# Matrix products that read and write their 512 columns in runs of 32 from two halves

## What is computed

```python
h = rmsnorm(x, norm_g)
aq, ak, av, ag, cq, ckv, kr, bg, mg = split(h @ w_in)
oa = rmsnorm(diff_attention(aq, ak, av, positions)) * (1 - lam_init)     # 8 heads
ya = (oa * silu(ag)) @ w_oa
q, kv = rmsnorm(cq) @ w_uq, rmsnorm(ckv) @ w_ukv
ob = mla_attention(q, kv, rope(kr))                                      # 8 heads
yb = (ob * silu(bg)) @ w_ob
merged = sigmoid(ga) * ya + sigmoid(gb) * yb                             # ga, gb = split(mg)
out = rmsnorm(x + merged @ w_out, final_g)
```

## Time and profile before

| | |
|---|---|
| median of the runs | 1429.43 us |
| the profiled execution's own time | 1430.07 us |
| its span from first to last instruction | 1428.1 us |
| TensorE matmul busy, share of the span | 99% |
| VectorE, ScalarE, GpSimd busy | 71%, 49%, 2% |
| mean granted TensorE clock | 0.998 |

### The profile page before, as it was taken

The page is one execution under the profiler, slowest core; times in us unless marked ns, Lnnn a source line. Parts: engine busy times, 40 slices in busy tenths (PEclk is TensorE's granted clock), DMA queues, the critical chain, the costliest instruction groups (busy, mean ns, idle before and its releaser), DMA issues.

```text
span 1428.1 us, 17872 instructions
## 1 busy us (share of the span) xinstructions
PE 1412.6 (99%) x6604; PEld 1174.5 (82%) x6604; DVE 1014.9 (71%) x1376; ACT 703.4 (49%) x890; POOL 29.8 (2%) x52
## 2 busy tenths in 40 slices
PE   8999999999999999999999999999999999999997
PEld 7888888888888888888888878888888888888886
DVE  6967888887877768677767655666676354388966
ACT  7546334444343456665666667555564122224434
POOL 0000000000000000000000000000000000000000
PEclk9999999999999999999999999999999999999999
DMA  8439575767665642222232434322342544617674
GB/s 302 143 125 319 175 265 185 251 198 231 219 203 187 208 126 81 76 82 81 81 85 84 110 104 132 86 69 66 84 137 74 154 127 146 207 45 250 191 258 170
DMA packets 182975, 218.42 MB, mean 153 GB/s; under 512 B 19456, under 2 KB 133248, under 8 KB 182272
## 3 DMA queue, kind: packets, MB, share of 16 engines
q1 hardware_dynamic: 174304, 197.64, 44.4%
q10 hardware_dynamic: 8608, 19.93, 3.8%
HBM read 195.51 MB, written 22.02 MB: 152 GB/s over the span
## 4 chain that ended last, share of the span: by engine, by line
PE 91%; DVE 4%; DMA 2%; ACT 1%; SPq 1%; issue 1%; POOL 0%; DVEq 0%; POOLq 0%; ACTq 0%
PE duo L2098 28%; PE duo L2100 28%; PE duo L2099 28%; PE duo L2151 2%; DMA start_y<-start_columns 1%; PE duo L2125 1%; PE duo L2128 1%; SPq L609 1%; ACT m_hi L885 1%; PE duo L2142 1%; PE duo L2147 1%; PE duo L2144 1%; PE duo L2143 1%; PE duo L2146 1%; PE duo L2581 0%
## 5 line engine op out<-in xcount | busy, mean ns | idle before, releaser
L1374 DVE TENSOR_TENSOR w_lo<-w_raw,w_hi 128x1024 fp32r<-128x1024 f32 (+1 forms) x116 | 135.2, 1167 | 101.6 <-ACT w_hi L780 101.1
L2098 PE MATMUL duo<-h_hi,w_hi 128*128 128x512 f32 x512 | 201.8, 394 | 0.0
L2100 PE MATMUL duo<-h_hi,w_lo 128*128 128x512 f32 x512 | 199.6, 390 | 0.0
L2099 PE MATMUL duo<-h_lo,w_hi 128*128 128x512 f32 x512 | 199.6, 390 | 0.0
L885 ACT ACTIVATE m_hi<-m_raw 128x2048 fp32r<-128x2048 f32 (+1 forms) x66 | 115.5, 1752 | 147.8 <-PE duo L2100 79.4
L780 ACT ACTIVATE w_hi<-w_raw 128x1024 fp32r<-128x1024 f32 (+1 forms) x118 | 119.2, 1011 | 126.5 <-DMA w_raw<-in_w_ob_dram 65.7
L1491 DVE TENSOR_TENSOR m_lo<-m_raw,m_hi 128x2048 fp32r<-128x2048 f32 (+3 forms) x71 | 141.9, 2001 | 29.0 <-ACT m_hi L885 28.8
L2098 PE MATMUL duo<-m_hi,h_hi 128*128 128x512 f32 x368 | 144.6, 393 | 1.6 <-DVE h_lo L1527 0.8
L2100 PE MATMUL duo<-m_hi,h_lo 128*128 128x512 f32 x368 | 143.3, 389 | 0.0
L2098 PE MATMUL duo<-m_hi,s_hi 128*128 128x512 f32 x320 | 124.5, 389 | 0.0
L2100 PE MATMUL duo<-m_hi,s_lo 128*128 128x512 f32 x320 | 124.5, 389 | 0.0
(11 more groups left out here) (320 smaller groups left out, 2953.9 us busy)
## 6 DMA issues: line engine op xcount, KB each, us to landing
m_raw<-in_w_in_dram SPq DMA_DIRECT2D x110, 512.0 KB, 4.5
w_raw<-in_w_in_dram SPq DMA_DIRECT2D x132, 256.0 KB, 3.0
o_raw<-in_w_out_dram SPq DMA_DIRECT2D x32, 512.0 KB, 5.1
spare<-in_w_in_dram SPq DMA_DIRECT2D x17, 512.0 KB, 4.9
h_raw<-in_w_in_dram SPq DMA_DIRECT2D x17, 512.0 KB, 4.8
w_raw<-in_w_oa_dram SPq DMA_DIRECT2D x32, 256.0 KB, 3.4
sig<-gates SPq DMA_DIRECT2D x8, 1024.0 KB, 6.4
w_raw<-in_w_ob_dram SPq DMA_DIRECT2D x32, 256.0 KB, 3.3
```

The costliest lines, as they stand in the source:

```text
L1374: dve.tensor_tensor(w_lo[:, piece.slot, 0:cols], w_raw[:, piece.slot, 0:cols], w_hi[:, piece.slot, 0:cols].bitcast(F32), ALU.subtract).the ...
L2098: pe.matmul(dst, lhs_hi, rhs_hi, start=start, stop=False, skip_group_check=onto)
L2099: pe.matmul(dst, lhs_hi, rhs_lo, start=False, stop=False, skip_group_check=onto)
L2100: return pe.matmul(dst, lhs_lo, rhs_hi, start=False, stop=stop, skip_group_check=onto)
```

## The change

All products of `three`, both score functions, the rotary keys and the feature sums go through a new helper, `multiply`, which rearranges the moving operand and the output in the same way. The 512 columns are taken as two halves of 256; the instruction goes through columns 0 to 31 of the first half, 0 to 31 of the second, 32 to 63 of the first, and so on: 16 runs of 32 (8 runs for the 256-column products). Reading and writing use the same order, so each output column gets the sum that it got before, at the same address. Where the moving operand already has two halves in separate places, these are the two halves. Stationary operands, semaphores, waits, the number and order of instructions, transposes and the other engines' code stay. The second product of the groups is accumulated in the banks as before.

```diff
--- before.py
+++ after.py
@@ -37,6 +37,9 @@
 LAM_INIT = 0.8 - 0.6 * math.exp(-0.3 * 0)
 SLOPE0, SLOPE_RATIO = 2.0 ** (-8.0 / HEADS), 2.0 ** (-8.0 / HEADS)
 NORM_EPS, SUBLN_EPS = 1e-6, 1e-5
+
+
+RUN = 32
 
 
 SLOTS = 4
@@ -2093,11 +2096,21 @@
 
         @block.tensor
         def _(pe):
+            def by_turns(columns):
+                if len(columns.shape) == 3:
+                    return columns.rearrange("p j (c r) -> p c j r", r=RUN)
+                return columns.rearrange("p (j c r) -> p c j r", j=2, r=RUN)
+
+            def multiply(dst, lhs, rhs, start, stop, onto=False):
+                return pe.matmul(
+                    by_turns(dst), lhs, by_turns(rhs), start=start, stop=stop, skip_group_check=onto
+                )
+
             def three(dst, lhs_hi, lhs_lo, rhs_hi, rhs_lo, start, stop, onto=False):
 
-                pe.matmul(dst, lhs_hi, rhs_hi, start=start, stop=False, skip_group_check=onto)
-                pe.matmul(dst, lhs_hi, rhs_lo, start=False, stop=False, skip_group_check=onto)
-                return pe.matmul(dst, lhs_lo, rhs_hi, start=False, stop=stop, skip_group_check=onto)
+                multiply(dst, lhs_hi, rhs_hi, start=start, stop=False, onto=onto)
+                multiply(dst, lhs_hi, rhs_lo, start=False, stop=False, onto=onto)
+                return multiply(dst, lhs_lo, rhs_hi, start=False, stop=stop, onto=onto)
 
             def tile(piece, c0, width=P):
                 return w_hi[:, piece.slot, c0:c0 + width], w_lo[:, piece.slot, c0:c0 + width]
@@ -2122,10 +2135,10 @@
                 q = slice(t * P, (t + 1) * P)
                 for m, dst in enumerate((a, b)):
 
-                    pe.matmul(dst[:, :], qa[:, m, q], ka[:, m, :], start=True, stop=False)
+                    multiply(dst[:, :], qa[:, m, q], ka[:, m, :], start=True, stop=False)
                 for m, dst in enumerate((a, b)):
 
-                    last = pe.matmul(dst[:, :], qa[:, m, q], ka_lo[:, m, :], start=False, stop=True)
+                    last = multiply(dst[:, :], qa[:, m, q], ka_lo[:, m, :], start=False, stop=True)
                 last.then_inc(scored, 1)
 
             def scores_b(h, t, prev):
@@ -2139,12 +2152,12 @@
                     pe.wait_ge(v_kept, TOK + VB_COPIES)
                 q = slice(t * P, (t + 1) * P)
                 dst = SC[t][:, :]
-                pe.matmul(dst, q_hl[:, 0, q], k_hl[:, 0, :], start=True, stop=False)
-                pe.matmul(dst, q_hl[:, 0, q], k_hl[:, 1, :], start=False, stop=False)
-                pe.matmul(dst, q_hl[:, 1, q], k_hl[:, 0, :], start=False, stop=False)
-
-                pe.matmul(dst, qr_hl[:, q], kr_hi[:, :], start=False, stop=False)
-                pe.matmul(dst, qr_hl[:, q], kr_lo[:, :], start=False, stop=True).then_inc(scored, 1)
+                multiply(dst, q_hl[:, 0, q], k_hl[:, 0, :], start=True, stop=False)
+                multiply(dst, q_hl[:, 0, q], k_hl[:, 1, :], start=False, stop=False)
+                multiply(dst, q_hl[:, 1, q], k_hl[:, 0, :], start=False, stop=False)
+
+                multiply(dst, qr_hl[:, q], kr_hi[:, :], start=False, stop=False)
+                multiply(dst, qr_hl[:, q], kr_lo[:, :], start=False, stop=True).then_inc(scored, 1)
 
             def turn(src, dst, done):
                 for k in range(TOK):
@@ -2174,8 +2187,8 @@
                 last.then_inc(pv_done, 1)
 
             def feature_sums(done):
-                pe.matmul(TR[:, :], ones_sq[:, :], vT_hi[:, :], start=True, stop=False)
-                pe.matmul(TR[:, :], ones_sq[:, :], vT_lo[:, :], start=False, stop=True).then_inc(done, 1)
+                multiply(TR[:, :], ones_sq[:, :], vT_hi[:, :], start=True, stop=False)
+                multiply(TR[:, :], ones_sq[:, :], vT_lo[:, :], start=False, stop=True).then_inc(done, 1)
 
             pe.wait_ge(cst_in, 16)
             pe.wait_ge(ones_set, 5)
@@ -2453,10 +2466,10 @@
                     both = w_hi[:, piece.slot, k * P:(k + 1) * P]
                     high = w_hi[:, piece.slot, k * P:k * P + B_ROPE]
                     if kt == 0:
-                        pe.matmul(ACC[1][:, :], both, h_hi[:, kt, :], start=True, stop=False)
-                    last = pe.matmul(ACC[1][LOW, :], high, h_lo[:, kt, :], start=False, stop=False)
+                        multiply(ACC[1][:, :], both, h_hi[:, kt, :], start=True, stop=False)
+                    last = multiply(ACC[1][LOW, :], high, h_lo[:, kt, :], start=False, stop=False)
                     if kt:
-                        last = pe.matmul(ACC[1][:, :], both, h_hi[:, kt, :], start=False, stop=kt == KT - 1)
+                        last = multiply(ACC[1][:, :], both, h_hi[:, kt, :], start=False, stop=kt == KT - 1)
                 last.then_inc(used, 1)
 
             def tail(q):
```

## The result

The changed kernel takes 1479.59 us, the kernel before 1429.47 us in the same comparison: a ratio of 1.0348 with a 95% interval of 1.033 to 1.0366, 50 us slower. The forecast was no change.

The account below looks back on a forecast made before the run. TensorE's queue of products was taken as the bound; 1430.07 us profiled plus 0 for 6144 products, with the runs' median 0.64 us lower, gave 1429.5 us. The whole range was 1352 to 1468 us, holding 0.87.

Parts of the forecast that it names:

- What bounds the kernel: Whole kernel: a queue of TensorE products, priced by the step between starts, 226.7 ns for 512 columns, 120.0 for 256.
- The reading side: Moving operand of each product: fifteen jumps at 512 columns, seven at 256, taken as 0; bounds 0 and 6.25 ns a product.
- The writing side: Output bank of each product: the same jumps, taken as 0; bounds 0, 6.25 ns a product, or below nothing.
- The slower rival: Every product: each jump costs a period or more; 1467 us at one period (chance 0.15), 1504 at two (more than one: 0.13).
- The 0.13 that the range left out above: Chance given to a price of more than one period a jump, on either side; 1504 us at two periods.
- The faster rival: Between products: alternating halves hides the 13.3 ns; all gone 1354 us (chance 0.12), half about 1392 us (part gone 0.06).
- the 13.3 ns: Time every product was taken to cost beside streaming its columns at 0.4167 ns each, whatever its length.
- The disturbed stretches: Steps after each four transposes, ten in 2.32 us instead of 2.27: another order might clear this, about 1425 us; chance 0.04.
- What stays: Weight loads, instruction number, semaphores, product order, result places, other engines' reads, DMAs and the 8 us tail expected unchanged.

Follow-up runs that it names:

- the first bench: Kernel before with 22 groups of 30 unneeded products behind its last, differing in columns, reading or writing order and tile width; 512 columns: 226.7 ns side by side, 236.7 in runs of 32.
- fix16: Kernel before plus groups of 30 unneeded products, moving operand read in runs of 16 from four parts 512 columns apart, all beginning at a multiple of 64; step 242.0 ns.

## Why the prediction was wrong, point by point

**What bounds the kernel** was right: TensorE's steps, all but without cover. 10.0 ns on 5760 products would be 57.6 us; 50 appeared, for the two reasons given with the result, and only the 4.4 us of shorter waits is cover.

**The reading side** is the step that failed. I took 0 for fifteen jumps because the products with two runs of 256 showed none for one. The row was right and was the wrong neighbour. Its jump goes from one multiple of 64 to another, so it keeps the round, as do the runs of 64; it could not show what a jump that breaks it costs. The bounds I put, 0 and one period a jump (6.25 ns), were too narrow: measured are 10.0 ns at 512 columns, and nothing at 256.

**The writing side** was right with 0, by the run that writes in turns alone, but by luck: the row I argued from was one of reading, and on the reading side the same argument failed.

**The slower rival** had the direction and the place, and named that no row showed sixteen runs; its form was wrong. A price for each jump would have given 233 and 123 ns; measured are 236.7 and 119.2. Its 1467 us is 13 us short, and the range ended there at 1468 us. The 0.13 that the range left out above is where the time fell.

**The faster rival** is out: no order read faster than side by side, but for about 1 ns at 256 columns. Its 1354 us isn't worked out either: 82 us are added up, and no row gives the 6 us taken off. What I said against it, that the 13.3 ns look like a price of the instruction or of its change of weights, is half right. They shrink with the stationary tile at 256 columns (13.3, 10.0 and 6.7 ns for 128, 96 and 64 stationary columns, and 6.7 again for 32) and don't at 512.

**The disturbed stretches** after transposes didn't get shorter; they got longer by less than the others. In the kernel before they are the settling that the first bench shows; in the changed kernel a product pays the price of its turns there as elsewhere.

**What stays** stayed: weight loads, transposes, the other engines, the tail.

Shown by runs: that it is the reading; that neither the number of jumps nor, for runs of 16 and more, their length decides; that the start of a run modulo 64 columns, against the end of the one before, does; that the stationary tile's place relative to the moving operand's matters with the same period. Argued, not shown: that the two streams of one engine, moving operand and next stationary tile, get in each other's way in the memory that both are read from, and that side by side they fall into a round in which they don't. For it are the shifted tiles and the series of steps in which a group settles. Against it, as the whole account, is that runs of 32 and of 16 took 236.7 and 240.0 ns also with 32 stationary columns, whose load is over after 109 ns. The Trainium skill, "TensorE: Matmul & The Clock Gate", section "Step-by-step: what each phase is for", has two independent read ports, so that loading weights takes nothing from a running product; the shifted tiles speak against that for these operands. Open is why the price comes in only beyond 256 columns with a tile of 128 (256 columns side by side take 120.0 ns there, which is already the slow pace), why breaking the round eight times costs as much as fifteen times while four quarters in turn (twelve breaks) cost 6.7 ns, and why narrow tiles slow 512 columns side by side.

## What to carry to other kernels

Where TensorE is the bound, look at the step between starts: a few nanoseconds in the way one product reads are some per cent of the kernel. Moving operands of float32r may jump as long as each run begins at the same place modulo 64 columns at which the last one ended, and the first columns of the moving operand and the stationary tile should agree modulo 64; the order of the output in the bank is free. This is shown for 512 columns (the jumps for 384 too), a stationary tile of 128, and writes in runs of 16 or more. And before a row is used as a bound for something new, ask in which property it is like the new thing: here it was the jump that was alike, and the place it led to that counted.

## What the runs showed of the hardware that I had not expected

- A shift of 32 columns in either operand costs 6 to 7 ns on 226.7; the same shift in both costs nothing (226.7 once settled).
- A group that starts out of step settles at 226.7 ns within ten products, through one and the same series of steps (234, 233, 236, 224, 231, 236, 228, 233, 231 ns) or the end of it.
- Products of float32r have two steps between which all these forms lie: 226.7 ns and 240.0 ns at 512 columns, with runs of 16 from two halves at the upper one whatever the tile; only runs of 8 and 4 went above it (243.3 and 250.7), and fix16 (242.0).
- 256 columns take 120.0 ns and 512 take 226.7, so two products of 256 cost 13.3 ns more than one of 512, but 448 columns cost 206.7, 6.7 more than 13.3 ns beside 0.4167 ns a column.
- Fewer stationary columns don't make a product of 512 columns shorter: 226.7, 230.0, 230.1 and 231.8 ns for 128, 96, 64 and 32.
